# One score pass of a latent attention, split into two 64-row products that stand on different rows of TensorE

## The reference, cut to what matters

```
q = concat(q_nope[.., 64], rope(q_rope[.., 32])) * 96 ** -0.5
k = concat(k_nope[.., 64], rope(k_rope[.., 32], shared by all heads))
s = einsum('bqhd,bkhd->bhqk', q, k)          # 8 heads x 1024 x 1024 scores
p = softmax(s, axis=-1)
out = einsum('bhqk,bkhd->bqhd', p, v)
```

## Time and profile before

| | us |
|---|---|
| median of 3 runs | 1717.63 (1717.46 to 1717.9) |
| the profiled execution's own time | 1716.55 |
| its span, first to last instruction | 1714.8 |
| PE busy in the span | 1685.3 |
| DVE / ACT / POOL busy in the span | 794.8 / 586.3 / 507.9 |
| the stretch from the first to the last MLA scores | 1314.4 to 1519.7 |

### The profile page before, as it was taken

One profiled execution on the slowest core, in us unless ns is written; L12 is line 12 of the kernel. 1 busy time (PEld: TensorE's weight loads), 2 busy tenths in 40 slices (PEclk: granted clock), 3 DMA queues, 4 the chain that ended last, 5 costly groups with the idle time before them and its releaser, 6 DMA issues.

```text
span 1714.8 us, 22451 instructions
## 1 busy us (share of the span) xinstructions
PE 1685.3 (98%) x8753; PEld 1412.5 (82%) x8753; DVE 794.8 (46%) x1214; ACT 586.3 (34%) x1337; POOL 507.9 (30%) x400
## 2 busy tenths in 40 slices
PE   7999999999999999999999999999999999999998
PEld 6778778889878787888978889788787999988886
DVE  4330366344352213554166541645521888855714
ACT  5101456334333102441135310442113777741211
POOL 6125033023333333021220223015313744534310
PEclk9999999999999999999999999999999999999999
DMA  5113022233267422113131232227465525226332
GB/s 204 50 64 108 13 62 70 87 118 93 74 217 268 117 62 59 50 50 85 56 84 38 72 82 60 69 54 266 139 227 162 143 61 139 53 68 212 108 114 98
DMA packets 99290, 178.20 MB, mean 104 GB/s; under 512 B 16200, under 2 KB 36080, under 8 KB 99056
## 3 DMA queue, kind: packets, MB, share of 16 engines
q1 hardware_dynamic: 63280, 95.31, 20.0%
q10 hardware_dynamic: 35904, 81.44, 13.6%
HBM read 115.49 MB, written 48.63 MB: 96 GB/s over the span
## 4 chain that ended last, share of the span: by engine, by line
PE 95%; DVE 2%; ACT 1%; DMA 1%; issue 0%; SPq 0%; POOL 0%; ACTq 0%; POOLq 0%; DVEq 0%
PE ps L1193 23%; PE ps L1107 15%; PE ps L813 14%; PE ps L1045 5%; PE ps L1360 5%; PE ps L1300 5%; PE ps L1241 4%; PE ps L947 4%; PE ps L1330 3%; PE ps L1313 3%; PE ps L868 3%; PE ps L1209 2%; PE ps L1222 2%; PE ps L999 2%; PE ps L972 1%; PE ps L846 1%
## 5 line engine op out<-in xcount | busy, mean ns | idle before, releaser
L700 POOL TENSOR_SCALAR w_hi<-w_stage 128x1024 fp32r<-128x1024 f32 (+3 forms) x140 | 126.6, 911 | 997.7 <-PE ps L1193 361.1
L707 POOL TENSOR_TENSOR w_lo<-w_stage,w_hi 128x1024 fp32r<-128x1024 f32 (+3 forms) x140 | 270.1, 1937 | 8.9
L1193 PE MATMUL ps<-h2T_hi,w_hi 128*128 128x512 f32 x384 | 156.5, 408 | 0.7 <-ACT gate_tiles L1608 0.7
L1107 PE MATMUL ps<-h2T_hi,w_hi 128*128 128x512 f32 x384 | 154.2, 402 | 0.3 <-issue 0.3
L1193 PE MATMUL ps<-h2T_hi,w_lo 128*128 128x512 f32 x384 | 152.0, 396 | 0.0
L1107 PE MATMUL ps<-h2T_hi,w_lo 128*128 128x512 f32 x384 | 151.6, 395 | 0.0
L1193 PE MATMUL ps<-h2T_lo,w_hi 128*128 128x512 f32 x384 | 151.2, 394 | 0.0
L1107 PE MATMUL ps<-h2T_lo,w_hi 128*128 128x512 f32 x384 | 151.1, 393 | 0.0
L1735 ACT ACTIVATE probs_dil<-probs_dil,dil_stats_out 128x256 f32<-128x256 f32 (+2 forms) x192 | 87.6, 457 | 135.4 <-DVE dil_stats_out L2301 135.4
L1300 PE MATMUL ps<-k_mla,q_mla 128*128 128x512 f32 x384 | 104.0, 406 | 0.0
L2393 DVE TENSOR_REDUCE small<-ps 128x1 f32<-128x1024 f32 x64 | 77.7, 1214 | 54.8 <-PE ps L1300 54.8
(11 more groups left out here) (296 smaller groups left out, 3814.1 us busy)
## 6 DMA issues: line engine op xcount, KB each, us to landing
w_stage<-in_w_in SPq DMA_DIRECT2D x76, 512.0 KB, 3.9
rope_swapped<-rope_in SPq DMA_DIRECT2D x192, 64.0 KB, 2.0
w_stage<-in_w_out SPq DMA_DIRECT2D x16, 512.0 KB, 3.8
gate_scr<-gate_tiles ACTq DMA_DIRECT2D x16, 512.0 KB, 3.5
gates<-gate_scr ACTq DMA_DIRECT2D x32, 256.0 KB, 3.6
dil_scr<-dil_out SPq DMA_DIRECT2D x96, 64.0 KB, 1.6
dil_nums<-dil_scr ACTq DMA_DIRECT2D x24, 256.0 KB, 4.0
x_back<-in_x ACTq DMA_DIRECT2D x8, 512.0 KB, 3.6
```

The source lines that it names most:

```text
L700: last = nc.gpsimd.tensor_scalar(hi_, raw_, 1.0, 0.0, ALU.mult, ALU.add)
L707: last = nc.gpsimd.tensor_tensor(lo_, raw_, hi_.bitcast(F32), ALU.subtract)
L1107: m = pe.matmul(ps[:, gate_bank(u), :], a[:, s, k, P * m_:P * m_ + P], b[:, k, COLS * n:COLS * n + COLS], start=(k == 0 and j == 0), stop= ...
L1193: m = pe.matmul(bank, a, b, start=(k == 0 and i == 0), stop=(k == KT - 1 and i == 2))
```

## The change: what it does

The third pass is no longer two matmuls of 128 rows, half of them zero. It is two matmuls of 64 rows. The first uses rows 0 to 63: the high plain queries as before, with the low keys 0 to 511. The second uses rows 64 to 127: the low keys 512 to 1023 now lie there, in the place of the zeros, and the high plain queries must lie there a second time. For the query tiles 0 to 3 these go into columns 512 to 1023 of plane 1 of K, which are free now, and for tiles 4 to 7 into new tiles `q_mla_again`. The two matmuls go into different banks of PSUM.

The load of a head has 13 DMAs in place of 10 (15 in place of 12 for heads 0 and 1): the low keys come in two halves, and two loads of the high queries are added. The zeroing of K falls away, so that GpSimd has two memsets fewer.

```diff
-    sb("gap_p_mla", [P, S], F32, b2)
+    q_again = [sb("q_mla_again_1", [P, 2, COLS], F32R, b2)]
...
     pm0 = sb("p_mla_0", [P, S], F32, b2)
+    q_again.insert(0, sb("q_mla_again_0", [P, 1, COLS], F32R, b2))
...
+    def q_twice(h):
+
+        return heads_k[h % 2][HD:P, 1, COLS:S], q_again[h % 2][HD:P, 0, :]
...
-            moves += [(K[0:HD, part, :], kn_d[part, nope]) for part in range(2)]
+            moves += [(K[0:HD, 0, :], kn_d[0, nope])]
+            moves += [(K[HD * n:HD * n + HD, 1, 0:COLS], kn_d[1, nope, COLS * n:COLS * n + COLS]) for n in range(HALF)]
+            moves += [(q_twice(h)[n].bitcast(F32), qn_d[0, nope, COLS * n:COLS * n + COLS]) for n in range(HALF)]
...
-            for i, (x_, r0) in enumerate(((heads_q[h], HD + MLA_R), (heads_k[h], HD))):
-                if h or i:
-                    pool.wait_ge(*after("heads_zeroed", 2 * h + i))
-                nc.gpsimd.memset(x_[r0:P, 1, :].bitcast(F32), 0.0).then_inc(sem("heads_zeroed"), 1)
+            if h:
+                pool.wait_ge(*after("heads_zeroed", h))
+            nc.gpsimd.memset(heads_q[h][HD + MLA_R:P, 1, :].bitcast(F32), 0.0).then_inc(sem("heads_zeroed"), 1)
...
-            passes = ((0, 0), (1, 0), (0, 1))
-            for j, (a, b) in enumerate(passes):
+            for a in range(2):
                 for n in range(HALF):
-                    m = pe.matmul(ps[:, 2 * (i % 2) + n, :], Q[:, a, q], K[:, b, COLS * n:COLS * n + COLS],
-                                  start=(j == 0), stop=(j == 2))
+                    pe.matmul(ps[:, 2 * (i % 2) + n, :], Q[:, a, q], K[:, 0, COLS * n:COLS * n + COLS], start=(a == 0), stop=False)
+            again = q_twice(h)[qt // 4][:, P * (qt % 4):P * (qt % 4) + P]
+            for n, x_ in enumerate((Q[0:HD, 0, q], again)):
+                m = pe.matmul(ps[:, 2 * (i % 2) + n, :], x_, K[HD * n:HD * n + HD, 1, 0:COLS], start=False, stop=True)
             m.then_inc(sem("m_scored"), 1)
```

More of the change, by code:

```diff
@@ L556, in hybrid_blocks_kernel @@
     for h_ in range(H1):
-        loads[h_ % 2] += 16 * (10 + 2 * (h_ < 2))
+        loads[h_ % 2] += 16 * (13 + 2 * (h_ < 2))
         head_total.append(loads[h_ % 2])
@@ L728, in mla_loop @@
             zero_rows(1)
-            pool.wait_ge(*after("heads_zeroed", 4))
+            pool.wait_ge(*after("heads_zeroed", 2))
             for k in range(n_t):
@@ L1293, in m_scores @@
             if qt == 0:
-                pe.wait_ge(*after("heads_zeroed", 2 * min(h, 1) + 2))
+                pe.wait_ge(*after("heads_zeroed", min(h, 1) + 1))
                 pe.wait_ge(*after(f"head_in{h % 2}", head_total[h]))
             Q, K, q = heads_q[h % 2], heads_k[h % 2], slice(P * qt, P * qt + P)
-            passes = ((0, 0), (1, 0), (0, 1))
-            for j, (a, b) in enumerate(passes):
+            for a in range(2):
                 for n in range(HALF):
-                    m = pe.matmul(ps[:, 2 * (i % 2) + n, :], Q[:, a, q], K[:, b, COLS * n:COLS * n + COLS],
-                                  start=(j == 0), stop=(j == 2))
+                    pe.matmul(ps[:, 2 * (i % 2) + n, :], Q[:, a, q], K[:, 0, COLS * n:COLS * n + COLS], start=(a == 0), stop=False)
+            again = q_twice(h)[qt // 4][:, P * (qt % 4):P * (qt % 4) + P]
+            for n, x_ in enumerate((Q[0:HD, 0, q], again)):
+                m = pe.matmul(ps[:, 2 * (i % 2) + n, :], x_, K[HD * n:HD * n + HD, 1, 0:COLS], start=False, stop=True)
             m.then_inc(sem("m_scored"), 1)
```

## The result

| | before | after |
|---|---|---|
| median of the runs, us | 1717.55 (4 runs) | 1725.7 (4 runs) |
| ratio, 95% interval | | 1.0048 (1.0037 to 1.006) |
| the profiled execution's own time, us | 1716.55 | 1723.68 |
| its span, us | 1714.8 | 1721.5 |

The changed kernel is slower by 8.15 us, 0.48%. Run again on another occasion it had 1727.36 us against 1717.69, a ratio of 1.0055 (1.0042 to 1.0067). Forecast were 1726.6 us, in 1722 to 1734.

What follows compares the result with a forecast made beforehand. The MLA loop was taken as bound by TensorE alone. 9.4 us less 0.2 for the start and 0.3 for the wait is 8.9, rounded to 9, giving a median of 1726.6 us, range 1722 to 1734.

Steps and rivals of the forecast that it cites:

- the main term: Third pass of the MLA loop: 0.16 us more in each of 59 steps, 9.4 us.
- Two small terms: Taken off the loss: 0.2 us won at the loop's start, 0.3 us less waiting ahead of a transpose.
- The step: One MLA loop iteration: 0.16 us more (held to 0.14 to 0.18), 3.38 us against 3.22.
- a change of the row count: Into or out of 64 rows: 0.09 to 0.10 us emptying, 0.11 us uncovered load, about 0.20 us, two per step.
- The pair's stream: The two 64-row matmuls of the third pass run side by side, 0.21 us once streaming, as float32 pairs did.
- The number of steps: Of 64 loop steps, 59 (5 to 63) pay in full; in the first five the longer scores are hidden.
- The one wait in the middle: TensorE's 0.6 us pause ahead of a transpose shrinks by 0 to 0.6 us; 0.3 taken.
- The start of the loop: Key-tile memset on POOL goes, first transposes come earlier: 0.2 us gained, between 0 and 0.4.
- The sum: Whole kernel: 9.4 less 0.2 and 0.3, 8.9, rounded to 9 us slower; chance 0.80.
- The serial pair: Rival: the two 64-row matmuls run one after the other, 0.37 us more a step, 1738.9 us; chance 0.09.
- The gain without a price for the change of mode: Rival: at both seams around L1308 a change costs nothing, 0.23 us a step saved, 1704.1 us; chance 0.06.
- The loads: Three more DMAs a head, load 1.6 us longer, covered by 15 us of slack: nothing taken.

Runs made afterwards that it cites:

- the pair twice: The changed kernel with its two 64-row matmuls issued twice in a row before going back to 128 rows: 1739.65 us, ratio 1.0129 to the kernel before.
- the two orders tried: The changed kernel with the 64-row matmuls of two steps put side by side, behind the transposes: 1735.23 us; ahead of the transposes: 1728.51 us.

## Why the prediction was right

The mechanism and the size of the main term hold. Two small terms were off, by 0.3 us each and in opposite directions; that they cancel is luck, but both are small beside the 9.4 us of the main term.

- **The step.** Forecast 0.16 us more, 3.38 in place of 3.22: measured 3.38. The seams borrowed from the float32 scores of another stage held for float32r: 0.31 forecast 0.32, 0.43 forecast 0.42, 0.22 forecast 0.23. The pair ran side by side, which was the open point.
- **What is paid for.** The prediction says that "a change of the row count" costs about 0.20 us. That is too wide: 128 to 96 rows cost nothing of the kind, 0.007 us a step; 128 to 64 did.
- **The pair's stream.** It was taken as 0.21 us; a steady pair takes 0.23 (the pair twice). This did not change the sum, since the way out, 0.42 to 0.43 us in all, was read as one piece.
- **The number of steps.** Steps 5 to 63 pay. From the start of step 5 to that of step 63 it was 187.51 us (1330.99 to 1518.50) and is 196.36 (1328.81 to 1525.17), 8.85 more. 58 steps at 0.163 (3.383 less 3.22) are 9.45; the rest is the next point.
- **The one wait in the middle.** Forecast: 0.3 us less. It was a real wait, and it stands ahead of a transpose, as in the earlier trace rows. ScalarE issues the loads of the dilated output in iteration 32 and comes late for one step. Before and after, PE around it:

```profile
1424.39 1.63 PE L1300 MATMUL ps<-k_mla,q_mla 128*128 128x512 f32 x6
...
1428.33 1.64 PE L1300 MATMUL ps<-k_mla,q_mla 128*128 128x512 f32 x6
```

```profile
1426.95 1.18 PE L1305 MATMUL ps<-k_mla,q_mla 128*128 128x512 f32 x4
...
1430.42 1.19 PE L1305 MATMUL ps<-k_mla,q_mla 128*128 128x512 f32 x4
```

  That step was 3.94 us, 0.72 over the others, and is 3.47, 0.09 over. The longer steps absorb 0.63 us of it, twice what was taken. In the repeated run 0.20 us of it was left (1430.77 to 1434.35 is 3.58 us).

- **The start of the loop.** Forecast: 0.2 us won, because the memset of the key tile is gone. This step of the prediction fails. In the changed kernel POOL scales right after one memset (compare), and the transposes start at 1322.26, 10.17 us after the first scores, where it was 10.50 (1314.41 to 1324.91): 0.33 us earlier, near the 0.36 that had been worked out as possible.

```profile
1312.09 1.09 PE L1305 MATMUL ps<-k_mla,q_mla 128*128 128x512 f32 x4
...
1322.26 1.09 PE L1320 MATMUL ps<-ident,p_mla 128*128 128x128 f32 x8
...
1325.34 1.16 PE L1320 MATMUL ps<-ident,p_mla 128*128 128x128 f32 x8 [0.39 <-DVE pT_mla_lo L2387]
...
1328.81 1.19 PE L1305 MATMUL ps<-k_mla,q_mla 128*128 128x512 f32 x4
```

  But the second transposes come 3.08 us later in place of 2.61, and they wait for VectorE. Its maximum of step 1, before and after:

```profile
1322.99 1.22 DVE L2393 TENSOR_REDUCE small<-ps 128x1 f32<-128x1024 f32 x1 [4.33 <-PE ps L1300]
```

```profile
1320.81 1.23 DVE L2400 TENSOR_REDUCE small<-ps 128x1 f32<-128x1024 f32 x1 [4.50 <-PE ps L1308]
```

  It starts 8.58 us after the first scores before, and 8.72 after, since the scores of step 0 ahead of it are longer (the scores of step 1 start at 6.99 us before, at 7.15 after). From there to the reciprocal of step 2 VectorE needs 5.06 us in both kernels (1322.99 to 1328.05, 1320.81 to 1325.87). So from the second transposes on VectorE sets the pace and not POOL, and the longer scores of step 0 are not hidden, as the prediction had them. Step 5 starts 16.72 us after the first scores, before 16.58 (the repeated run: 16.72). The gain was given back, and 0.14 us with it.

- **The sum.** In the profiled executions the loop and its start cost 8.85 + 0.14, and the last step 0.16, together 9.15 us. Forecast were 9. The two profiled executions differ by only 7.13 us, because the changed one came to its first scores 2.3 us earlier (1312.09 for 1314.41), which is scatter and no part of the change. The medians differ by 8.15 and, repeated, by 9.67.
- **The rivals.** The serial pair: its price is the kernel with both matmuls on rows 0 to 63, 1740.7 us, forecast 1738.9. The gain without a price for the change of mode: refuted by every seam, 64 of 64 steps. By the span model of the Trainium skill (page "TensorE: Matmul & The Clock Gate", section "Measured speedup vs the span model") the tiles of a pack start some 4 ns apart, and this trace agrees, with 0.01 us. The model has no term for the way in and out. The Trainium skill's page "TensorEngine Tiling (Array Packing)", section Key Properties, says that a change of tiling mode drains TensorE. The runs agree that the change costs time, 0.40 us for each stay (4.01 us a step with two stays), but not how much of it is a drain. The loads: nothing that can be told (0.9999).

What is not settled: how the 0.40 us split. The rows suggest, at each end, about 0.1 us for emptying the array and about 0.1 for the load that is not ahead, but no experiment took one away without the other. Why the load is not fetched ahead is open too.

## What to carry to other kernels

The numbers are those of this kernel: float32r, 512 columns, 64 of 128 rows, the clock at 1.00. Two matmuls on half of the array's rows do run at once and cost as much as one, so packing saves one matmul; going to half rows and back costs 0.40 us, 1.7 matmuls of 512 columns. Count the stays, not the matmuls: pack only where two or more pairs stand in one stay, and where the work that must be moved together for that has slack in the chain behind it. Don't judge by TensorE's busy time, which rose here; count its matmuls per microsecond, or look at what stands ahead of the weight loads.

## What the runs showed that was not expected

- Going from 128 rows to 96 costs next to nothing, 3.22 us a step, while 64 rows cost 0.40 us a stay. The prediction had put the price on any change of the row count.
- Two 64-row matmuls on the same rows and different banks run one after the other (0.33 us between the starts), and a pair on different rows streams in 0.23 us, the same as a 128-row float32r matmul, not the 0.21 us of the float32 pairs of 256 columns.
- The shared stay would win 0.07 us in two steps over the kernel before (6.37 us for 6.44). In the two orders tried, waits took 0.46 and 0.26 us: 6.83 and 6.63 us.
- VectorE, and not the memset on POOL, sets the pace at the start of the loop, so that taking the memset away won nothing.
